# Turning the feed-forward units by DMA instead of on TensorE, in a two-layer float32 kernel

## The reference, cut to what matters

```python
m = rms_norm(h, mlp_pre_gain[l])
z = jnp.square(jax.nn.relu(jnp.einsum("bsd,df->bsf", m, w_up[l])))   # f = 8192
z = jnp.einsum("bsf,fd->bsd", z, w_down[l])
...
gu = h2 @ w_gu                                                       # 2 x 5632 wide
x = x + (jax.nn.silu(gu[..., :D_FF_2]) * gu[..., D_FF_2:]) @ w_down
```

## Time and profile before

| | |
|---|---|
| median of 3 runs | 2540.2 us |
| profiled execution, its own time | 2540.15 us |
| its span, first to last instruction | 2538.0 us |
| TensorE busy | 2512.3 us (99%) |
| VectorE busy | 1422.9 us (56%) |
| ScalarE busy | 1296.9 us (51%) |
| mean granted TensorE clock | 0.998 |

### The profile page before, as it was taken

How to read it: one execution, slowest core, us unless ns; L and a number is a source line. 1 busy time by engine, 2 the same in 40 slices (tenths; PEclk the granted TensorE clock), 3 DMA queues, 4 the chain that set the end, 5 groups by cost and what they waited for, 6 DMA issues and landing times.

```text
span 2538.0 us, 31944 instructions
## 1 busy us (share of the span) xinstructions
PE 2512.3 (99%) x11347; PEld 2085.4 (82%) x11347; DVE 1422.9 (56%) x1500; ACT 1296.9 (51%) x1669; POOL 67.1 (3%) x78
## 2 busy tenths in 40 slices
PE   8999999999999999899999999999999999999999
PEld 7888878888888888788888888888888888888887
DVE  5888565455455455665566645555554544545554
ACT  5886554444444444454475544445544444444443
POOL 0010000000000000011100000000000000000000
PEclk9999999999999999999999999999999999999999
DMA  7897656666665656465555566665656666666665
GB/s 241 236 268 215 199 175 187 207 196 198 196 187 189 192 175 197 149 191 190 189 173 174 174 191 191 190 191 182 190 176 202 191 195 190 186 192 195 190 183 166
DMA packets 249290, 488.52 MB, mean 192 GB/s; under 512 B 15364, under 2 KB 15932, under 8 KB 248924
## 3 DMA queue, kind: packets, MB, share of 16 engines
q1 hardware_dynamic: 244460, 470.14, 59.7%
q0 software_dynamic: 4688, 16.93, 3.1%
q10 hardware_dynamic: 32, 0.01, 0.0%
HBM read 474.42 MB, written 4.47 MB: 189 GB/s over the span
## 4 chain that ended last, share of the span: by engine, by line
PE 98%; ACT 1%; DVE 0%; DMA 0%; issue 0%; POOL 0%; SPq 0%; ACTq 0%; DVEq 0%
PE acc L409 32%; PE acc L411 32%; PE acc L410 32%; PE tp L426 2%; PE po L601 0%; PE sc L571 0%; DMA h<-x_dram 0%; ACT yb L818 0%; PE tp L589 0%; DVE w_lo L1026 0%; PE po L603 0%; ACT w_hi L684 0%; ACT ev L691 0%; PE sc L426 0%; ACT junk L718 0%
## 5 line engine op out<-in xcount | busy, mean ns | idle before, releaser
L1026 DVE TENSOR_TENSOR w_lo<-raw,w_hi 128x1024 fp32r<-128x1024 f32 x888 | 1075.7, 1224 | 919.8 <-ACT w_hi L684 916.6
L684 ACT ACTIVATE w_hi<-raw 128x1024 fp32r<-128x1024 f32 x888 | 931.1, 1060 | 957.3 <-PE acc L411 932.4
L409 PE MATMUL acc<-w_lo,a_hi 128*128 128x512 f32 x2304 | 904.4, 393 | 1.2 <-DVE w_lo L1026 1.2
L411 PE MATMUL acc<-w_hi,a_lo 128*128 128x512 f32 x2304 | 898.3, 390 | 0.0
L410 PE MATMUL acc<-w_hi,a_hi 128*128 128x512 f32 x2304 | 897.4, 390 | 0.0
L411 PEld LDWEIGHTS acc<-w_hi,a_lo 128*128 128x128 f32 x2304 | 433.1, 188 | 91.2
L409 PEld LDWEIGHTS acc<-w_lo,a_hi 128*128 128x128 f32 x2304 | 433.4, 188 | 90.4 <-issue 2.6
L410 PEld LDWEIGHTS acc<-w_hi,a_hi 128*128 128x128 f32 x2304 | 433.6, 188 | 88.1
L409 PE MATMUL acc<-w_lo,b_hi 128*128 128x512 f32 x1120 | 436.7, 390 | 0.3 <-DVE w_lo L1026 0.3
L411 PE MATMUL acc<-w_hi,b_lo 128*128 128x512 f32 x1120 | 435.8, 389 | 0.0
L410 PE MATMUL acc<-w_hi,b_hi 128*128 128x512 f32 x1120 | 435.8, 389 | 0.0
(11 more groups left out here) (167 smaller groups left out, 910.6 us busy)
## 6 DMA issues: line engine op xcount, KB each, us to landing
raw<-w_in_dram SPq DMA_DIRECT2D x272, 512.0 KB, 4.4
raw<-w_down_dram SPq DMA_DIRECT2D x216, 512.0 KB, 4.7
raw<-w_gu_dram SPq DMA_DIRECT2D x176, 512.0 KB, 4.4
raw<-w_up_dram SPq DMA_DIRECT2D x128, 512.0 KB, 3.8
raw<-w_out_dram SPq DMA_DIRECT2D x64, 512.0 KB, 4.3
raw<-w_branch_dram SPq DMA_DIRECT2D x32, 512.0 KB, 3.8
tap_sum<-tap_add POOLq DMA_DIRECT2D x20, 512.0 KB, 7.1
skew_dram<-line_dram POOLq DMA_DIRECT2D x12, 192.0 KB, 4.7
```

The source lines that it names most:

```text
L409: nc.tensor.matmul(out, xh, wl, start=s == 0 and k == 0, stop=False)
L411: mm = nc.tensor.matmul(out, xl, wh, start=False, stop=s == n - 1 and k == KS - 1)
L684: nc.scalar.activation(w_hi[:, ring], raw[:, ring], ACT.Copy).then_inc(hi_ready, 1)
L1026: nc.vector.tensor_tensor(w_lo[:, ring], raw[:, ring], w_hi[:, ring].bitcast(F32), ALU.subtract).then_inc(lo_ready, 1)
```

## The change

26 of the 27 turns of the feed-forward parts leave TensorE; the last one (the third pair of the last, shorter block) stays. In their place:

- VectorE, after `zz`, parts its 32-bit words into a plane of low and a plane of high 16-bit halves, one copy for each half of the positions (`part_planes`).
- ScalarE issues two DMA transposes, one for each half of the positions, 128 x 1024 16-bit elements (256 KB) each, after its second tick of the next unit (`turn_planes`).
- One tick later ScalarE waits for both, joins the planes into 32-bit words again (two copies, `joined`), and rounds these into `b_hi` (two copies) (`join_planes`).
- VectorE subtracts into `b_lo` after its third tick (`split_joined`).
- The loops over blocks on ScalarE and SyncE are written out in Python; those of TensorE and VectorE in the first layer stay.

```diff
@@ PE, mlp_block
-                    slots(gj, u + j, 0, 2, a_hi, a_lo, pair=j % 2)
-                    if j:
-                        turn(zz, (z_ready, z + j), (split_lo, sp_ + 2 * j - 3))
-                    slots(gj, u + j, 2, SPU, a_hi, a_lo, pair=j % 2)
+                    slots(gj, u + j, 0, SPU, a_hi, a_lo, pair=j % 2)
...
@@ ScalarE
+            def turn_planes(n):
+                for tk in range(TT):
+                    act.wait_ge(planes_ready, 2 * n + tk + 1)
+                    act.dma_start(
+                        planesT.rearrange("p t k s -> p (t k) s")[:, :, tk * P:(tk + 1) * P],
+                        planes[:, tk].rearrange("p t c -> p (t c)"), transpose=True
+                    ).then_inc(planes_turned, 16)
+
+            def join_planes(n, lo_done, dst, k0):
+                act.wait_ge(planes_turned, 32 * (n + 1))
+                act.wait_ge(split_lo, lo_done)
+                for q in range(2):
+                    nc.scalar.activation(
+                        joined[:, 2 * q:2 * q + 2, :].rearrange("p k s -> p (k s)").bitcast(
+                            U16).rearrange("p (s t) -> p t s", t=2),
+                        planesT[:, :, 2 * q:2 * q + 2, :].rearrange("p t k s -> p t (k s)"),
+                        ACT.Copy).then_inc(join_done, 1)
+                for q in range(2):
+                    act.wait_ge(join_done, 2 * n + q + 1)
+                    nc.scalar.activation(dst[:, k0 + 2 * q:k0 + 2 * q + 2, :],
+                                         joined[:, 2 * q:2 * q + 2, :], ACT.Copy
+                                         ).then_inc(split_hi, 1)
...
+                    if 1 <= v <= NCH:
+                        ticks(g, RING + v * SPU, RING + v * SPU + 2)
+                        turn_planes(X_MLP + b * NCH + (v - 1))
+                        ticks(g, RING + v * SPU + 2, RING + v * SPU + 3)
+                        join_planes(X_MLP + b * NCH + (v - 1), S_MLP + b * (2 * NCH) + 2 * (v - 1),
+                                    b_hi, 4 * (v - 1))
+                        s_from = 3
+                    ticks(g, RING + v * SPU + s_from, RING + v * SPU + s_to)
...
-                    split(T_MLP + b * (2 * NCH) + 2 * j, b_hi, 4 * j)
...
@@ VectorE
+            def part_planes(n, z):
+                dve.wait_ge(z_ready, z)
+                for tk in range(TT):
+                    nc.vector.tensor_copy(planes[:, tk], zz[:, tk].bitcast(U16).rearrange(
+                        "p (c t) -> p t c", t=2)).then_inc(planes_ready, 1)
+
+            def split_joined(split0, hi, lo, k0):
+                for q in range(2):
+                    dve.wait_ge(split_hi, split0 + (q + 1))
+                    nc.vector.tensor_tensor(lo[:, k0 + 2 * q:k0 + 2 * q + 2, :],
+                                            joined[:, 2 * q:2 * q + 2, :],
+                                            hi[:, k0 + 2 * q:k0 + 2 * q + 2, :].bitcast(F32),
+                                            ALU.subtract).then_inc(split_lo, 1)
...
+                    if 1 <= v <= NCH:
+                        ticks(g, RING + v * SPU, RING + v * SPU + 3)
+                        split_joined(S_MLP + b * (2 * NCH) + 2 * (v - 1), b_hi, b_lo, 4 * (v - 1))
...
-                    split(S_MLP + b * (2 * NCH) + 2 * j, b_hi, b_lo, 4 * j)
+                    part_planes(X_MLP + b * NCH + j, b * NCH + (4 + j + 1))
```

More of the change, by code:

```diff
@@ L121, in build_program @@
                    at("tap_add2", 184, [P, 4, S])]
+        planes = at("planes", 144, [P, TT, 2, W], U16)
+        planesT = at("planesT", 148, [P, 2, 4, S], U16)
+        joined = at("joined", 152, [P, 4, S])
         qkT = at("qkT", 144, [P, 2 * NH, S])
@@ L325, in _ @@
                          src[:, ks(part * RING + s), unit * W:(unit + 1) * W])
[L326 removed]
+            for b in range(FF1 // D):
                 g = G_MLP + b * (2 * NCH * SPU)
[L328 to L330 removed]
+                for v in range(2 * NCH):
                     for s in range(SPU):
[L332 to L335, removed]
+                        c0 = v % NCH * W
+                        src = (w_up[:, ks(s), b * D + c0:b * D + c0 + W] if v < NCH
+                               else w_down[:, b * KT + KS * s:b * KT + KS * s + KS, c0:c0 + W])
+                        load(s, g + v * SPU + s, src)
             with sp.Fori(0, 3 * NCH) as j:
@@ L359, in _ @@
                     load(s, G_OUT2 + j * SPU + s, src[:, ks(s)])
-            with sp.Fori(0, 2) as b:
+            for b in range(2):
                 g = G_FF + b * (3 * NCH * SPU)
[L362 to L365, removed]
+                for v in range(3 * NCH):
                     for s in range(SPU):
[L367 to L371, removed]
+                        if v < 2 * NCH:
+                            c0 = v % 2 * FF2 + b * D + v // 2 * W
+                            src = w_gu[:, ks(s), c0:c0 + W]
+                        else:
+                            c0 = (v - 2 * NCH) * W
+                            src = w_dn2[:, b * KT + KS * s:b * KT + KS * s + KS, c0:c0 + W]
+                        load(s, g + v * SPU + s, src)
             for j in range(6):
@@ L533, in mlp_block @@
                     split0 = sp_ if j == 0 else None
[L534 to L537, removed]
+                    slots(gj, u + (NCH + j), 0, SPU, b_hi, b_lo, split0=split0, pair=j % 2)
             mlp_block(0, True)
@@ L876, in _ @@
             mlp_block(0)
-            with act.Fori(1, FF1 // D - 1) as b:
+            for b in range(1, FF1 // D - 1):
                 mlp_block(b)
@@ L1003, in ff_block @@
                     hi_ = RING + s0 + down_slots - (RING if last and j == NCH - 1 else 0)
-                    ticks(g, RING + s0, hi_)
+                    if j == 0 and not last:
+                        ticks(g, RING + s0, RING + s0 + 2)
+                        turn_planes(X_FF + b * NCH + pairs - 1)
+                        ticks(g, RING + s0 + 2, RING + s0 + 3)
+                        join(pairs - 1)
+                        ticks(g, RING + s0 + 3, hi_)
+                    else:
+                        ticks(g, RING + s0, hi_)
                     s0 += down_slots
@@ L1012, in ff_block @@
                     evacuate(j % 2, g + s0, ev[:, j % 2])
-            with act.Fori(0, 2) as b:
+            for b in range(2):
                 ff_block(G_FF + b * (3 * NCH * SPU), b, NCH, SPU, False)
@@ L1298, in mlp_block @@
                 for j in range(NCH):
-                    ticks(g, RING + (NCH + j) * SPU,
-                          RING + (NCH + j + 1) * SPU - (last and j == NCH - 1))
+                    unit_ticks(NCH + j, 0, SPU - (last and j == NCH - 1))
                     if last and j:
```

72 lines of the change are left out of this document (51 added, 21 removed).

## The result

| | before | after |
|---|---|---|
| median | 2540.47 us (6 runs, 2538.3 to 2541.35) | 2601.36 us (6 runs, 2595.16 to 2616.21) |
| profiled execution, its time and its span | 2540.15, 2538.0 us | 2606.07, 2604.2 us |
| mean granted TensorE clock | 0.998 | 0.985 |

The change makes the kernel slower: ratio 1.0247, 95% interval 1.022 to 1.0274. I had forecast 2516.8 us and faster. The time lies inside the range, on the side of the rivals.

A forecast was written before the change was run, and what follows sets the result against it. The prediction took TensorE, busy 99% of the span, as the bound: 2540.15 us less 23.4 us for 26 removed turns, with all added work hidden, gave 2516.8 us; the range was 2513 to 2620 us.

The forecast's parts named there:

- What is removed: On TensorE's path: 26 turns at 0.90 us each go, 23.4 us (bounds 20.5 and 27.0).
- X, from the nearest rows: Step pricing the transposes by a same-size weight load plus a second issue: 4.8 us, ends 3.4 and 14.5.
- X: Time from a unit's first transpose issue on ScalarE until both transposes have landed; taken as 4.8 us.
- the stall: TensorE's wait for late weights: 20 (X - 6.7) + 6 (X - 6.3) past the limits; none at 4.8 us.
- The limits of X: Largest X the ring of four weight slots hides: 6.7 us for slot 7, 6.3 for `b_lo` in 6 units.
- Where the wait would show: TensorE's wait for `w_lo` would grow equally in each of 26 units, in slot 7, or slot 6 for `b_lo`.
- Rival 1: Planes land late among weight loads, X above 7.5 up to 11; at 9, 62 us stall, 2579 us; chance 0.18.
- Rival 2: Transposes go in 256-byte packets at 99 ns, X 14.5: 205 us stall, 2722 us; chance 0.15.
- Rival 3: Each transpose's issue holds ScalarE for Y; at Y = 3, X 8.6, 52 us stall, 2569 us; chance 0.07.
- Rival 4: Transposes only partly hidden, X of 6.7 to 7.5: 2529.6 us at 7.1; chance 0.08.
- Rival 5: Transposes push weight loads' landing beyond 8.6 us; at 2 us beyond, 52 us lost, 2569 us; chance 0.04.
- The written-out loops: Writing out the loops changes SyncE's work between issues by a 0.03 us move: nothing.

The follow-up runs named there:

- e10: e5 with transposes issued one tick sooner; in the 6 units a first down unit needs, slot 7's tick precedes the join; halves rounded when joined: 2518.0 us.
- e9: e5 with the 6 units that a block's first down unit needs turned on TensorE as before the change: 2520.9 us.
- e8: The changed kernel with the two DMAs of a unit as plain copies in rows of 2048 bytes, planes joined unturned: 2527.4 us.
- e3: The changed kernel with weight loads halved to 256 KB in the blocks with transposes but the last: 2544.5 us.
- e7: The changed kernel with weight loads cut to 64 KB in the blocks with transposes but the last: 2523.7 us (one run).
- e2: The changed kernel with the two DMAs of a unit as plain copies in rows of 256 bytes: 2541.5 us.
- e4: The changed kernel with join and subtraction moved from the third to the sixth tick in 20 units: 2560.5 us.
- e6: The kernel before, with only the loops over blocks of SyncE and ScalarE written out: 2539.1 us.
- e5: e4 with TensorE's loop over the blocks of the first feed-forward part written out: 2549.5 us.
- e13: The changed kernel without DMA transposes, with 12 unread turns, each after a wait for `zz`, in TensorE's looped blocks: 2540.0 us.
- e15: e13 with waits and unread turns also in the written-out first block, ahead of TensorE's loop: 2529.9 us.

## Why the prediction was wrong, step by step

- **What is removed, 23.4 us: right.** With nothing in the way (e10) the profiled execution is 2516.85 us, forecast 2516.8. An agreement that close is luck: the median is 2518.0, 22.3 us below the kernel before, or 0.86 us a turn. e9 gives 20 turns: 2520.9 against 2522.
- **The step that failed is "X, from the nearest rows".** I took the load row, 4.8 us. It is 9.25. The reason that I gave for the row (same bytes, same kind of queue, no arithmetic) was good for a plain copy in long rows (e8: 5.6 us, no stall), not for a transpose. The term that it fed, the stall, was set at 0 and measured 51.4 us.
- **The limits of X: right in kind, 0.5 to 0.8 us too low.** I let the issue wait for the end of the tick before it. It went out when that tick started (577.75 beside 577.73), at T + 5.5. The parting took 0.69 us a copy instead of 1.23, the join 1.34 instead of 1.06. Measured, the limits are 7.5 us for slot 7 and, in most tight units, 6.8 for `b_lo`. In e3 (X of 7.6) the time is back within 4 us of the kernel before, two loop stops included.
- **Where the wait would show: right.** Slot 7, or `b_lo` for slot 6 in six units. It showed in 22 units and not in all 26, and not by the same amount in each: in the other four X was 6.3 to 7.0 us, below the limit.
- **Rival 1, the planes come late: this is what happened,** in the place it named and for the reason it gave, the engines shared with the loads (e3, e7). Its price at X = 9 was 62 us of stall, 2579 us, against 51.4 us and 2601: it lacked the clock (some 25 us) and the loop stops (8).
- **Rival 2, small pieces: the pieces are there, not their price.** ScalarE's queue has 54944 packets where the copies in long rows have 7520, 256 bytes each. One takes 0.039 x 16 x 2604.2 / 54944 = 30 ns, not the 99 that I lent it; in e2, with 54112 packets of the same size in plain copies, it is 19 ns.
- **Rival 3, the issue holds ScalarE: half true.** Y, the length of one issue, is 1.33 us, above the 0.37 of a load and below the 2.5 from which it would decide alone. Two longer issues make 1.3 us of the 2.4 that X is longer with transposes than with plain copies in the same rows.
- **Rival 4, partly hidden: no.** An X near its 6.7 to 7.5 us came only in e2 (6.9) and e3 (7.6), and there the loss is small, as it said.
- **Rival 5, starving loads: no** (e4). Loads land there after 4.4 us in the median, as before.
- **The written-out loops: right for ScalarE and SyncE** (e6). That taking code out of TensorE's program would make its own loop stop for 8 us and some clock was in no step and no rival; writing that loop out takes 11 us off (e5).
- **The two pages.** The Trainium skill (Advanced Engine Details and Errata, X-Bar Transpose) has transposing DMAs as fast as regular ones. The runs here disagree as to the time that ScalarE waits: the same bytes in the same rows took X = 6.9 us plain and 9.25 transposed; bandwidth by itself was not measured. The Trainium skill (VectorE: DVE Perf Modes, the three transpose paths) has 1309 ns for a 128x128 block. With the loads nearly gone, the 16 blocks of a unit took 5.2 us in all, issues included, so they don't go one after another at that price.

## What to carry to other kernels

When a transfer takes over work from an engine, price its latency in the traffic of the place where it will run, with its own issue time, and put the wait for it as late as the first reader allows: moving the join by three ticks here was worth 41 us at no cost. A wait inside an engine that feeds a ring is free up to a sharp limit and then paid in every round, and where the fed engine is TensorE, slower matmuls behind the stops come on top (here about 25 us on 63). After taking instructions out of an engine's program, look at its hardware loops in the trace; a stop with no releaser where a loop goes back, with a higher packet count on the instruction queue, was cured here by writing the loop out.

## What the runs showed of the hardware

- A DMA transpose of 128 x 1024 16-bit elements holds the issuing ScalarE for 1.33 us, a plain copy of the same bytes 0.57 to 0.69 (medians, e8 and e2). Two issued behind each other took 4.0 us in one place of e10, with ScalarE idle.
- It moves in packets of about 256 bytes, and with little other traffic (e7) lands 3.4 us after its issue; among weight loads that keep the 16 engines some 60% busy, after 6.8 us, and up to 10.8.
- A loop of TensorE's sequencer can cost 2 to 5 us each time it goes back or nothing, by what stands ahead of it in the program (e13 against e15). Where it stops, its body is loaded anew, 17 instruction packets of 16 KB in two passes; where it doesn't, none.
- A TensorE that had been idle for 4.85 us worked at 1.2 GHz for some 5 us after it (granted clock 0.50 in the first 3 us). Behind an idle time of 1.34 us the next matmul took 0.50 us and those after it 0.39 to 0.40 again.
